# Last projection of a two-block transformer kernel as seven block products, with weight sums made ahead by GpSimd

## The reference, cut to what matters

```python
gate, up = jnp.split(h @ ffn_w_up[l], 2, axis=-1)
gate = _causal_dwconv(gate, ffn_conv_w[l], ffn_conv_b[l])
f = jax.nn.gelu(gate, approximate=True) * up                      # 1024 x 2816
x = x + _rmsnorm(f @ ffn_w_down[l], norm_ffn_post[l]).astype(dt)  # 2816 x 1024 weights
```

## Time and profile before

| | us |
|---|---|
| median of 3 runs | 3133.95 (3129.6 to 3135.03) |
| the profiled execution, its own time | 3125.92 |
| its span, first to last instruction | 3124.1 |
| outside the span | 1.8 |
| mean granted TensorE clock | 0.935 |
| PE busy | 2770.0 (89%) |
| DVE busy | 2019.5 (65%) |
| ACT busy | 1377.1 (44%) |
| POOL busy | 529.9 (17%) |

### The profile page before, as it was taken

How to read it: one execution, slowest core, us unless ns; L and a number is a source line. 1 busy time by engine, 2 the same in 40 slices (tenths; PEclk the granted TensorE clock), 3 DMA queues, 4 the chain that set the end, 5 groups by cost and what they waited for, 6 DMA issues and landing times. The chain is left out here.

```text
span 3124.1 us, 42344 instructions
## 1 busy us (share of the span) xinstructions
PE 2770.0 (89%) x14382; PEld 2306.4 (74%) x14382; DVE 2019.5 (65%) x2489; ACT 1377.1 (44%) x2158; POOL 529.9 (17%) x342
## 2 busy tenths in 40 slices
PE   5999996799789999995899979667977799999998
PEld 5887785687768888884777768556855688887886
DVE  3996417674479999996652357664346888885344
ACT  4122327622268888885423125563335333332233
POOL 1233120020012111121222100001001443430000
PEclk9999998999889999998999989788688999999999
DMA  3112226043199999996413220302022122223322
GB/s 104 34 47 75 81 71 219 20 149 110 60 365 417 412 417 412 416 415 239 139 44 85 56 79 2 108 29 40 16 98 98 48 81 81 82 82 98 141 97 95
DMA packets 253445, 442.34 MB, mean 142 GB/s; under 512 B 34221, under 2 KB 153044, under 8 KB 253300
## 3 DMA queue, kind: packets, MB, share of 16 engines
q1 hardware_dynamic: 223972, 370.61, 33.3%
q10 hardware_dynamic: 20480, 39.85, 3.5%
q0 software_dynamic: 8848, 29.96, 2.9%
HBM read 359.54 MB, written 80.81 MB: 141 GB/s over the span
## 5 line engine op out<-in xcount | busy, mean ns | idle before, releaser
L2213 DVE TENSOR_TENSOR e_w_lo<-e_ring,e_w_hi 128x1024 fp32r<-128x1024 f32 x384 | 447.0, 1221 | 47.4 <-ACT e_w_hi L2140 47.4
L2140 ACT CAST e_w_hi<-e_ring 128x1024 fp32r<-128x1024 f32 x384 | 377.2, 1048 | 35.4 <-PE banks L2073 28.5
L2071 PE MATMUL banks<-e_w_hi,e_xT_hi 128*128 128x512 f32 x512 | 203.2, 397 | 0.0
L2073 PE MATMUL banks<-e_w_hi,e_xT_lo 128*128 128x512 f32 x512 | 200.5, 392 | 0.0
L2072 PE MATMUL banks<-e_w_lo,e_xT_hi 128*128 128x512 f32 x512 | 200.1, 391 | 0.0
L956 DVE SCALAR_TENSOR_TENSOR conv<-x_first,vectors,conv 128x1024 f32<-128x1024 f32 x120 | 186.5, 1555 | 9.8 <-issue 0.9
L940 POOL TENSOR_TENSOR p_w_lo<-p_w,p_w_hi 128x1024 fp32r<-128x1024 f32 (+1 forms) x48 | 111.5, 2323 | 338.7 <-ACT p_w_hi L866 338.7
L2349 PE MATMUL banks<-fd_w_hi,fd_s_hi 128*128 128x512 f32 x352 | 139.1, 395 | 12.3 <-DVE fd_s_lo L2447 12.3
L2621 PE MATMUL banks<-u_sums,u_w_hi 128*128 128x512 f32 (+1 forms) x364 | 140.0, 385 | 10.8 <-DVE u_sums L2800 9.5
L804 PE MATMUL banks<-h_hi,p_w_hi 128*128 128x512 f32 x352 | 141.2, 401 | 1.3 <-POOL p_w_lo L940 1.3
L2622 PE MATMUL banks<-u_sums,u_w_hi 128*128 128x512 f32 (+1 forms) x364 | 139.7, 384 | 0.0
(11 more groups left out here) (631 smaller groups left out, 7380.1 us busy)
## 6 DMA issues: line engine op xcount, KB each, us to landing
e_ring<-in_w_gate_e_dram SPq DMA_DIRECT2D x128, 512.0 KB, 6.4
e_ring<-in_w_up_e_dram SPq DMA_DIRECT2D x128, 512.0 KB, 7.0
e_ring<-in_w_down_e_dram SPq DMA_DIRECT2D x128, 512.0 KB, 5.5
u_w<-in_ffn_w_up_dram SPq DMA_DIRECT2D x44, 512.0 KB, 5.8
expert_results<-nothing SPq DMA_DIRECT2D x1, 16384.0 KB
expert_results<-e_y ACTq DMA_DIRECT2D x32, 512.0 KB, 7.7
p_w<-in_w_in_dram SPq DMA_DIRECT2D x24, 512.0 KB, 3.8
fd_w<-in_ffn_w_down_dram SPq DMA_DIRECT2D x42, 256.0 KB, 2.6
```

Of the source, the lines that this page charges most:

```text
L2071: mm(bank, xT_hi[:, b, k, :], w_hi[:, part, cols], start=(k == 0), stop=False)
L2073: last = mm(bank, xT_lo[:, b, k, :], w_hi[:, part, cols], start=False, stop=(k == KT - 1))
L2140: nc.scalar.copy(w_hi[:, part, :], experts.ring[:, slot, :]).then_inc(w_rounded, 1)
L2213: tt(w_lo[:, part, :], experts.ring[:, slot, :], w_hi[:, part, :].bitcast(F32), ALU.subtract).then_inc(w_split, 1)
```

## The change

1. **The last projection by seven block products** (`ffn_down` instead of `project_and_add` for tag `fd`). With `f` as 2x2 blocks (token halves by depth halves of 1408) and the weights as 2x2 blocks (depth halves by column halves of 512), the product is made from seven block products instead of eight (Winograd's form of Strassen's scheme). Each has 11 depth chunks and 4 token tiles, so there are 77 steps of 12 matmuls. The sums of blocks of `f` are formed in place by DVE (`form`, one tensor_tensor of 128x512 a step for steps 22 to 65), the sums of results by DVE out of PSUM. The ring has four slots for everything, operands of a step are 128x512 both, and the code is written out instead of looped.
2. **Four sums of weight blocks** (`w_sums`, 4 x 1408 x 512 in DRAM) are made in the first attention stage by `DownSums`: 11 turns, in each SP loads 1 MB of weights, POOL makes four 128x512 tensor_tensors, and SP stores 1 MB. The last projection reads these sums instead of weights in products 5, 6, 7 and 4.
3. The residual `x` is loaded in eight DMAs of 512 KB instead of one of 4 MB; the options `first`, `rows` and `head` of `project_and_add` are gone. Its other use (tag `o2`) stays as it was.

The diff, cut to its core:

```diff
-def soft_attention(K, tag, ..., turned_room, decay=None):
+def soft_attention(K, tag, ..., turned_room, decay=None, beside=None):
+        if beside is not None:
+            @block.sync
+            def _(sp):
+                beside.on_sync(sp)
+            @block.gpsimd
+            def _(pool):
+                for _ in range(beside.TURNS):
+                    beside.turn(pool)
+class DownSums:
+    TURNS = FFT // 2
+    def __init__(self, K, scope, sums):
...
+        self.raw, self.out = K.sb(scope, "t_raw", [P, 2, 2, D]), K.sb(scope, "t_out", [P, 2, 4, HALF])
+    def on_sync(self, sp):
...
+        load(0)
+        load(1)
+        for k in range(self.TURNS):
+            sp.wait_ge(self.made, 4 * k + 4)
+            sp.dma_start(target[:, k], self.out[:, k % 2]).then_inc(self.stored[k % 2], 16)
+            if k + 2 < self.TURNS:
+                load(k + 2)
+        for b in range(2):
+            sp.wait_ge(self.stored[b], 16 * ((self.TURNS + 1 - b) // 2))
+    def turn(self, pool):
...
+        pool.wait_ge(self.landed[k % 2], 16 * (k // 2 + 1))
+        if k >= 2:
+            pool.wait_ge(self.stored[k % 2], 16 * (k // 2))
+        tt(out[:, 0], b12, b11, ALU.subtract).then_inc(self.made, 1)
+        tt(out[:, 2], b22, b12, ALU.subtract).then_inc(self.made, 1)
+        pool.drain()
+        tt(out[:, 1], b22, out[:, 0], ALU.subtract).then_inc(self.made, 1)
+        pool.drain()
+        tt(out[:, 3], b21, out[:, 1], ALU.subtract).then_inc(self.made, 1)
+def ffn_down(K, f, head, rows, first, sums, y, src, out):
+    DEPTH, SLOTS, H = FFT // 2, 4, NT // 2
+    PRODUCTS = (1, 2, 5, 6, 7, 3, 4)
+    steps = [(i, k) for i in range(7) for k in range(DEPTH)]
+    LAST = len(steps) - 1
...
+            def load(n):
+                if n >= SLOTS + 2:
+                    sp.wait_ge(split, 2 * (n - SLOTS) + 1)
+                sp.dma_start(w[:, n % SLOTS, :], weight_rows(i, k)).then_inc(landed[n % SLOTS], 16)
...
+            for n in range(2, 6):
+                load_rows(n)
+                load(n)
+            for n in range(6, LAST + 1):
+                load(n)
+                if n < FFT:
+                    load_rows(n)
...
+                if n == 5 * DEPTH + SLOTS + 1:
+                    sp.wait_ge(split, 2 * 5 * DEPTH)
+                    load_x(0)
+            sp.wait_ge(formed, 4 * DEPTH)
+            load_x(1)
...
+            for n in range(LAST + 1 - SLOTS):              # PE
+                pe.wait_ge(split, 2 * n + 2)
+                for t in range(H):
+                    if k == 0 and m != 1 and m != 5:
+                        taken = {2: copied, 6: c11_kept, 7: u_made, 3: v_made, 4: c22_made}[m]
+                        pe.wait_ge(taken, t + 1)
+                    done = product(n, t, k == 0 and m in (1, 5, 6, 7), k == DEPTH - 1)
...
+            pe.wait_ge(split, 2 * LAST + 2)
+            for t in range(H):
+                for n in range(LAST + 1 - SLOTS, LAST + 1):
+                    done = product(n, t, False, n == LAST)
+                done.then_inc(ended, 1)
...
+            for n in range(LAST + 1):                      # ACT
+                fill(n)
+                if n == DEPTH - 1 + SLOTS - 1:
+                    for t in range(H):
+                        wait_end(act, 0, t)
+                        nc.scalar.activation(y[:, t, right], bank(0, t), ACT.Copy).then_inc(copied, 1)
...
+            root(0, H)
+            for t in range(H, NT):
+                act.wait_ge(c21_made, t - H + 1)
+                square(0, t, y[:, t, left])
+                root(t)
...
+            for n in range(LAST + 1):                      # DVE
+                form(n + 1)
+                rest(n)
...
+                if n == 4 * DEPTH - 1 + SLOTS - 1:
+                    dve.wait_ge(copied, H)
+                    for t in range(H):
+                        wait_end(dve, 3, t)
+                        tt(y[:, H + t, left], bank(3, t), y[:, t, right], ALU.add).then_inc(u_made, 1)
...
+                if n == LAST - 2:
+                    dve.wait_ge(squared, 3 * H)
...
+                    for t in range(H):
+                        times_gain(t, right, 3 * H)
+            dve.wait_ge(x_landed[0], 16 * H)
+            dve.drain()
+            for t in range(H):
+                add(t)
+            dve.wait_ge(x_landed[1], 16 * H)
+            for t in range(H, NT):
+                wait_end(dve, 6, t - H)
+                dve.drain()
+                tt(y[:, t, left], bank(6, t - H), y[:, t, left], ALU.add).then_inc(c21_made, 1)
+                dve.wait_ge(squared, 3 * H + t - H + 1)
+                stt(rstd[:, t:t + 1], ss[:, 0, t:t + 1], 1.0 / D, ss[:, 1, t:t + 1], ALU.mult, ALU.add).then_inc(meaned, 1)
+                times_gain(t, left, 3 * H + t - H + 1)
+                add(t)
```

More of the change, by code:

```diff
@@ L2259, in _, with project_and_add @@
                 split_w(*tail(used, j))
-def project_and_add(K, tag, srcT, depth, weight, gain_row, x, y, src, out, squares=False, first=None, rows=None, head=None):
+def project_and_add(K, tag, srcT, depth, weight, gain_row, x, y, src, out, squares=False):
     nc = K.nc
@@ L2278, in project_and_add @@
     pairs = depth // 2
-    row_landed = [K.sem(f"{tag}_row_landed{b}") for b in range(2)] if rows is not None else None
-    own = 16 if first is None else 0
     ahead = min(NT // 2 + 2, pairs - 1)
@@ L2284, in project_and_add @@
         w = K.sb(scope, f"{tag}_w", [P, 2, HALF])
-        opening = w if first is None else first
         w_hi, w_lo = (K.sb(scope, f"{tag}_w_{part}", [P, 4, HALF], F32R) for part in ("hi", "lo"))
@@ L2291, in project_and_add @@
         rstd = K.sb(scope, f"{tag}_rstd", [P, NT])
-        def source(c):
-            return head[:, c, :] if head is not None and isinstance(c, int) and c < 2 else srcT[:, c, :]
         @block.sync
@@ L2330, in _ @@
                     load(i + pairs, b, 1, i * 2 + b)
-            if first is not None:
-                sp.wait_ge(split, (pairs + NT // 2 - 1) * 4 + 8)
-                sp.dma_start(x[:], src.rearrange("(t p) d -> p t d", p=P)).then_inc(x_landed, 16)
             with sp.Fori(ahead, pairs) as i:
@@ L2403, in _ @@
             for b in range(2):
-                if first is None:
-                    act.wait_ge(landed[b], 16)
-                copy(w_hi[:, b, :], opening[:, b, :])
-                copy(s_hi[:, b, :], source(b))
+                act.wait_ge(landed[b], 16)
+                copy(w_hi[:, b, :], w[:, b, :])
+                copy(s_hi[:, b, :], srcT[:, b, :])
             with act.Fori(1, pairs) as i:
                 for b in range(2):
-                    if rows is not None:
-                        act.wait_ge(row_landed[b], i * 16)
                     fill(i, b, i * 2 + b)
```

219 lines of the change are left out of this document (184 added, 35 removed).

## The result

The changed kernel ran 4 times with a median of 3102.9 us (3101.63 to 3110.13), the kernel before 4 times with 3131.77 (3129.45 to 3135.03). The ratio is 0.9915 with a 95% interval of 0.9897 to 0.9933: 26.6 us less, between 21 and 32. The profiled execution took 3103.3 us with a span of 3101.5 and a mean granted clock of 0.931; that of before took 3125.92, so the two traces stand 22.6 us apart. The forecast was -19.6. Two of the ten executions of one later experiment (e4_sums_only: 3234.8 and 3355.5 us, at a granted clock of 0.85 and 0.81 where the others had 0.93) are left out of every figure.

The account below looks back on a forecast made before the run. PE was taken to bound the last projection, no single engine the first attention stage. Projection -29.6 us and attention +10 gave -19.6 from 3133.95, so 3114.3 us, range 3103 to 3130.

Parts of the forecast that it names:

- Step 44: Last projection, product 7 into product 6's banks: PE waits 0.3 us for DVE's first read and the hand-over.
- The gap ahead of the last four steps: Last projection: PE waits 2.3 us after step 72 for DVE's second rest, where it was 7.0 us.
- The tail: End of last projection: DVE's queue, not PE, ends it; 25.0 us where it was 30.0.
- DVE's delay: First attention stage: DVE instructions with two SBUF inputs wait for POOL's additions, 15 us in all.
- The share that reaches the end: First attention stage: about two thirds of DVE's delay lengthens the stage, +10 us, bounds 2 and 33.
- The turns: First attention stage: POOL's turns start at 527 us, take 8.2 each, end at 621, covered with 7 to spare.
- Rival (c): First attention stage: turns outlast the stage, gain gone from 11.0 us a turn, 3144 us at 12; chance 0.06.
- how it stands to the runs: Whole kernel: -19.6 us against the profiled execution, whose 8 us distance to the median is added, giving 3114.3 us.
- Rival (a): First attention stage: POOL disturbs little, DVE's delays fall into its waits, +2 us, 3106 us; chance 0.12.
- (b): First attention stage: 30 DVE meetings pay the lock in full, +27 to +33 us, 3131 to 3137; chance 0.12.
- (d): Last projection: the ring starves in the first 22 steps or between products, 10 us lost, 3124; chance 0.15.
- (e): Last projection: PE's pace does not carry over, so the stage gains nothing; held excluded, given no chance.

Follow-up runs that it names:

- e4_sums_only: The kernel before plus the weight sums in the first attention stage, which nobody reads; median 3136.2 us of 8 runs, ratio 1.0015.
- e5: The changed kernel with each POOL addition of 512 columns made as two of 256; 3096.54 us, one run.
- e6: The changed kernel with three of DVE's four early residual additions moved behind the first sums out of PSUM in the tail; 3103.97 us.
- e11: The changed kernel with POOL's additions halved to 256 columns and residual additions moved into DVE's gaps; median 3100.7 us of 4 runs, ratio 0.9900.
- e10: The changed kernel with only two loads and two stores, all 44 POOL additions kept, projection reading plain weight blocks; 3102.69 us, one run.
- e9: The changed kernel without POOL's data work: SP stores what it loaded, 11 loads and 11 stores stay; 3098.71 us, one run.
- e7: The changed kernel with the weight sums made in the second attention stage, in quarter-size turns over four buffers; 3128.5 us, ratio 0.9999.
- e1: The changed kernel without the 44 POOL additions, one POOL memset ahead instead, loads and stores kept; 3101.56 us, one run.
- e2: The changed kernel without loads and all but two stores; POOL clears a tile, then makes the 44 additions; 3112.85 us, one run.

## Why the prediction was right, and where it was off

**Direction and mechanism: right.** The projection gains what PE no longer does, the attention stage pays part of it back through DVE, and nothing else moves.

**The projection, term by term.** PE's first matmul comes 2.0 us after ACT's first instruction, before 2.9: 0.9 earlier (said: 0.8). 200.8 us to the end of step 72 (201.4). Step 44: 0.3 (0.3). The gap ahead of the last four steps: 2.05 (2.3). The tail: 25.5 (25.0), made of 6.95 to the first sum from the banks (6.4), 15.1 for four tiles (15.6) and 3.5 behind DVE's last (3.0). Together -30.1 (-29.6). Here the rule that a stage bound by one engine is priced by that engine's work and the waits at both its ends gave each term within 0.6 us. The slow matmuls at the start cost 200.8 - 198.6 - 0.3 = 1.9 us instead of 2.5; the first is 0.50 us long where it was 0.80.

**The attention stage: the mechanism right, the size 2 us too large.** The term that was mis-sized is DVE's delay: said 15 us, measured 10.0. The working had 20 meetings of 0.6 us, 12 in all, and then 3 more for a POOL instruction that itself waited and is met by DVE's next. The trace has 22 of 0.46 us. Such second meetings occur (L2509 at 530.54 above is met by DVE's next L1338, 1.17 us long where it takes 0.75), but they are within the 22: the number of meetings was about right, the wait in one was taken too long. What was lost was shared out, 10.0 us on DVE's side and 11.9 on POOL's. The share that reaches the end was said as two thirds and is 0.79, and it can be read better than it was: DVE's idle ahead of the row maxima gave 2.1 us, no more. In e5, e6, e11 the same sum (delay less what that idle gave) makes 4.7, 7.0 and 5.0, and the stage grew by 4.5, 6.7 and 5.0; in e10 it makes 7.8 and the stage grew by 8.3 against e9 (9.2 against before, whose 145.7 is the shortest of the undisturbed stages). Single stages differ by 2 us with nothing beside them, so these sums bear the reading out together and not to a tenth. The 13.2 us of waits of the earlier trace rows were then not slack for DVE: most of them, by this reading, are PE and ACT working on what DVE hands over, and they move along with a late DVE.

**The turns.** Said 527 for the first, 8.2 us a turn, the last store landed at 621; measured 526.4, 7.2, and a last store issued at 604.1 that takes 5.0 to land. The pace was too pessimistic since it took POOL's 7.6 us from a stage in which DVE leaves no gaps; here the 44 instructions are 1.55 us long on the mean, and after the first load POOL waited only 6.5 us for all the others. The DMA's half of the round was too long as well: a load landed 7.4 us after its issue, right behind the store's, where 8.7 were said for both. The cover is 17.8 us, where 7 were said. Rival (c) didn't occur, but it was well placed: e7 shows it with its full price of 30 us.

**The time itself.** Forecast 3114.3 with a range from 3103; the median is 3102.9, at its very end. Part of that is the kernel before, whose median is 3131.77 with a fourth run where the forecast started from 3133.95; by the ratio the change makes 3107.3 of that. By the marks the miss is small: -22.2 us (+7.9 - 30.1) against -19.6. The larger part is the step "how it stands to the runs": it took the profiled execution's distance to the median, 8 us, as a constant. It isn't one. The profiled execution of before lies 6 us below the median of its four runs, that of after at its median, and the middle of the kernel moves between 2243 and 2250 us with its code unchanged. The lower end of the range left 3 us for this, less than the 5.6 us by which four runs of before differ. Rival (a), 3106, was nearest in time and is wrong as a mechanism: of DVE's 10 us of delay 2 fell into its waits and 8 reached the end, where it had 2 reaching the end.

**Rivals.** (b) the lock paid in full: excluded, DVE paid a third of the 33 us. (d) a starving ring: excluded by 50.00 of 50.00 us at 298 GB/s, and between products by 0.3 us in all. (e) PE's pace: 0.2268 us for 0.2267.

## What to carry to other kernels

Price work on an idle engine by the instructions of its neighbour that it excludes, in the stage where it is put: 44 POOL additions cost 8 us beside DVE instructions with two SBUF inputs, some 5 us when cut in halves, and, cut in halves, no more than 2.5 us where DVE mostly reads PSUM. Then look at the queue that feeds it: a SP list in which a load waits for the store just issued made a turn 5.4 us instead of 3.5 and cost 30 us at the block's end; another order of loads and stores, begun a buffer deeper, mended it. When an experiment needs a harmless instruction (a memset), look in its own trace at what it did before reading the verdict.

## What the runs showed of the hardware that was not expected

- A POOL memset, which reads nothing, held up DVE's `tensor_scalar` with one SBUF input (e1: 128x4096 in 3.51 us; four fills of 64x1024 from 2.79 to 6.11 us), and a memset with additions behind it held the same four up to 9.02 us (e2). So the prediction's sentence that a DVE instruction with one SBUF input is spared doesn't hold for these fills; the row maxima out of PSUM were spared in every trace (47.1 to 47.6 us). The fill takes 0.69 us for 1024 columns where a tensor_tensor of as many takes 1.22. The Trainium skill (page "SBUF — State Buffer", section "Who interferes with whom") spares one SBUF input only outside DVE's 2-port modes, a condition that the prediction left out, and names these modes as contending with GpSimd; if this fill runs in one, which no run here shows by itself, the trace agrees.
- A 1 MB load issued right behind the 16 MB fill landed after 53.1 us, the others after 7.4 (median): it stood behind nearly all of the fill, and that delay moved POOL's work away from the early splits. In e2, where it didn't, the same additions cost 13.4 instead of 10.0 us of DVE.
- After a gap of 2.05 us PE's first matmul took 0.50 us and the following ones had the full pace, at a granted clock of 1.00 (3076 to 3086, after: the 2.4 GHz level). After 4.42 us several took 0.63, at 0.64 on the mean from 2873.2 to 2878; after 5.30 us the first took 0.80, at 0.50 from 2866.6 to 2870 in before (the 1.2 GHz level). That the length of the gap alone decides is not shown.
